# Differential attention: q and k rotated with rows exchanged by transfers within SBUF in place of products with a rotation matrix

## What is computed

```python
def partial_rope(x, cos, sin):            # ROPE_DIM 16 of each 64 channels
    half = ROPE_DIM // 2
    x1 = x[..., :half].astype(jnp.float32)
    x2 = x[..., half:ROPE_DIM].astype(jnp.float32)
    rot = jnp.concatenate([x1 * c - x2 * s, x2 * c + x1 * s], axis=-1)
    return jnp.concatenate([rot.astype(x.dtype), x[..., ROPE_DIM:]], axis=-1)
...
    q = partial_rope(q, cos, sin) * (DH ** -0.5)
    k = partial_rope(k, cos, sin)
...
        s = jnp.einsum('bhcqd,bhckd->bhcqk', q_blk, kt).astype(f32)
        pr = jax.nn.softmax(s, axis=-1)
        pd = pr[:, :, 0] - lam * pr[:, :, 1]
        return jnp.einsum('bhqk,bhkv->bhqv', pd.astype(vt.dtype), vt)
```

## Time and profile before

| | us |
|---|---|
| median of 3 runs (1713.19 to 1714.20) | 1713.61 |
| profiled execution, its own time | 1713.43 |
| its span, first to last instruction | 1711.7 |

### The profile page before, as it was taken

One profiled execution on the slowest core, in us unless ns is written; L12 is line 12 of the kernel. 1 busy time (PEld: TensorE's weight loads), 2 busy tenths in 40 slices (PEclk: granted clock), 3 DMA queues, 4 the chain that ended last, 5 costly groups with the idle time before them and its releaser, 6 DMA issues. The chain is left out here.

```text
span 1711.7 us, 30337 instructions
## 1 busy us (share of the span) xinstructions
PE 1665.2 (97%) x12956; PEld 1305.7 (76%) x12956; DVE 1062.3 (62%) x1509; ACT 725.0 (42%) x1092; POOL 97.0 (6%) x122
## 2 busy tenths in 40 slices
PE   9999999999999999999999999998899999999997
PEld 6666777778767888888888788874477878888887
DVE  6757588878657577576765762327786654343434
ACT  4344555534255443232314553245664553232323
POOL 0000000000000100000111000003100100000001
PEclk9999999999999999999999999999999999999999
DMA  6111231111155344446562232230001223232221
GB/s 220 63 61 68 83 117 40 40 40 47 34 209 185 123 160 147 150 167 212 207 211 77 84 111 62 84 104 0 1 2 62 99 92 106 87 101 97 99 98 50
DMA packets 50165, 171.18 MB, mean 100 GB/s; under 512 B 5600, under 2 KB 9056, under 8 KB 49264
## 3 DMA queue, kind: packets, MB, share of 16 engines
q1 hardware_dynamic: 40272, 133.00, 22.1%
q0 software_dynamic: 9760, 36.25, 6.2%
HBM read 160.84 MB, written 8.39 MB: 99 GB/s over the span
## 5 line engine op out<-in xcount | busy, mean ns | idle before, releaser
L378 PE MATMUL pair<-h_hi,w_hi 128*128 128x512 f32 x1008 | 404.1, 401 | 3.0 <-DVE w_lo L424 2.1
L380 PE MATMUL pair<-h_hi,w_lo 128*128 128x512 f32 x1008 | 392.8, 390 | 0.0
L379 PE MATMUL pair<-h_lo,w_hi 128*128 128x512 f32 x1008 | 392.7, 390 | 0.0
L424 DVE TENSOR_TENSOR w_lo<-w_raw,w_hi 128x1024 fp32r<-128x1024 f32 (+2 forms) x225 | 266.5, 1186 | 172.8 <-ACT w_hi L403 172.6
L403 ACT CAST w_hi<-w_raw 128x1024 fp32r<-128x1024 f32 (+2 forms) x225 | 222.1, 990 | 224.3 <-PE pair L380 219.6
L378 PEld LDWEIGHTS pair<-h_hi,w_hi 128*128 128x128 f32 x1008 | 189.3, 188 | 59.2 <-issue 19.0
L379 PEld LDWEIGHTS pair<-h_lo,w_hi 128*128 128x128 f32 x1008 | 189.4, 188 | 41.0 <-issue 4.1
L380 PEld LDWEIGHTS pair<-h_hi,w_lo 128*128 128x128 f32 x1008 | 189.2, 188 | 40.3
L378 PE MATMUL pair<-ff_f_hi,w_hi 128*128 128x512 f32 (+1 forms) x536 | 204.1, 381 | 0.6 <-DVE w_lo L424 0.6
L380 PE MATMUL pair<-ff_f_hi,w_lo 128*128 128x512 f32 (+1 forms) x536 | 203.5, 380 | 0.0
L379 PE MATMUL pair<-ff_f_lo,w_hi 128*128 128x512 f32 (+1 forms) x536 | 203.5, 380 | 0.0
(11 more groups left out here) (457 smaller groups left out, 2503.4 us busy)
## 6 DMA issues: line engine op xcount, KB each, us to landing
w_raw<-in_w_ff SPq DMA_DIRECT2D x128, 512.0 KB, 3.3
mod_w<-in_w_mod POOLq DMA_DIRECT2D x48, 512.0 KB, 3.7
w_raw<-in_w_in SPq DMA_DIRECT2D x22, 512.0 KB, 3.3
w_raw<-in_w_gate SPq DMA_DIRECT2D x16, 512.0 KB, 3.3
w_raw<-in_w_out SPq DMA_DIRECT2D x16, 512.0 KB, 3.3
w_raw<-in_w_rwkv SPq DMA_DIRECT2D x15, 512.0 KB, 3.2
w_raw<-in_w_da SPq DMA_DIRECT2D x12, 512.0 KB, 4.1
w_raw<-in_w_ple_gate SPq DMA_DIRECT2D x8, 512.0 KB, 3.2
```

The costliest lines, as they stand in the source:

```text
L378: nc.tensor.matmul(out, w_hi, x_hi, start=(k == 0), stop=False)
L379: nc.tensor.matmul(out, w_hi, x_lo, start=False, stop=False)
L380: last = nc.tensor.matmul(out, w_lo, x_hi, start=False, stop=(k == kt - 1))
L424: nc.vector.tensor_tensor(lo[:, s % SPLIT_SLOTS, 0:cols], pr.raw[:, w % RAW_SLOTS, 0:cols], hi[:, s % SPLIT_SLOTS, 0:cols].bitcast(F32), A ...
```

## The change

The eight products with `rot` go, with the matrix and its load. In their place SP copies rows within SBUF: for tile i four transfers of eight rows (16 KB each) bring rows 8 to 15 to 0 to 7, 0 to 7 to 8 to 15, and the same from row 64 on, from the tile into its slot of `turned`. The rest of `turned` is cleared once by GpSimd, ahead of its load of the table. The sign moves into the sine table, which the host lays out. VectorE's sine product reads `turned` and writes it back.

```diff
@@ the tables
+    sin[:, 0:8] *= -1
     out["rope_da"] = per_channel(np.tile(cos, (1, 2)), np.tile(sin, (1, 2)))
@@ DiffAttention
     def load(self, pool):
         nc, dram = self.pr.nc, self.pr.dram
+        for i in range(2):
+            nc.gpsimd.memset(self.turned[:, i, :], 0.0).then_inc(self.s["cleared"], 1)
         pool.dma_start(self.table[:, :, :], dram["rope_da"].rearrange("p (a t) -> p a t", a=2)).then_inc(self.s["table_in"], 16)
 
-    def load_rotation(self, pool):
-        pool.dma_start(self.rot[:, :], self.pr.dram["rot_da"]).then_inc(self.s["rot_in"], 16)
+    def swap(self, sp, i):
+
+        s = self.s
+        sp.wait_ge(s["tile_out"], i + 1)
+        if i < 2:
+            sp.wait_ge(s["cleared"], 2)
+        else:
+            sp.wait_ge(s["roped"], i - 1)
+        for row in (0, 8, 64, 72):
+            sp.dma_start(self.turned[row:row + 8, i % 2, :], self.Q[row ^ 8:(row ^ 8) + 8, DA_ORDER[i], :]).then_inc(s[f"swapped{i % 2}"], 16)
...
@@ DiffAttention.pe, k == 2
-            pe.wait_ge(s["tile_out"], i + 1)
-            if slot > DA_FIRST + 1:
-                pe.wait_ge(s["tr_out"], slot - DA_FIRST - 1)
-            elif i >= 2:
-                pe.wait_ge(s["sin_made"], i - 1 if i == 3 else i)
-            nc.tensor.matmul(self.turn_bank(i), self.rot[:, :], Q[:, DA_ORDER[i], :], start=True, stop=True).then_inc(s["rot_done"], 1)
@@ DiffAttention.pe, k == 6
-            if slot <= 8:
-                pe.wait_ge(s["sin_made"], slot)
-            elif slot <= 12:
+            if 9 <= slot <= 12:
                 pe.wait_ge(s["v_out"], slot - 8)
-            else:
+            elif u:
                 pe.wait_ge(s["tr_out"], u)
@@ DiffAttention.dve
-            dve.wait_ge(s["rot_done"], i + 1)
-            nc.vector.tensor_tensor(self.turned[:, i % 2, :], self.turn_bank(i), self.table[:, 1, :], ALU.mult).then_inc(s["sin_made"], 1)
+            dve.wait_ge(s[f"swapped{i % 2}"], 64 * (i // 2 + 1))
+            nc.vector.tensor_tensor(self.turned[:, i % 2, :], self.turned[:, i % 2, :], self.table[:, 1, :], ALU.mult)\
+                .then_inc(s["sin_made"], 1)
@@ DaIn
     def loads(self, sp):
         self.start_loads(sp)
+        for i in range(2 * DA_HEADS):
+            self.pr.stream(sp, self.jobs[i].weight + 7)
+            self.beside.swap(sp, i)
```

More of the change, by code:

```diff
@@ L88, in shape_constants @@
         "ident64": (i[:, None] % 64 == np.arange(64)[None, :]).astype(f),
-        "rot_da": rope_rotation((64, 8)),
         "rot_att": rope_rotation((64, 32)),
@@ L452, in __init__ @@
         self.sq = [self.table[:, 0, :], self.table[:, 1, :], self.turned[:, 0, :], self.turned[:, 1, :]]
-        self.probT, self.oT, self.rot, self.small, self.lam = (
-            scratch("da_" + k, shape) for k, shape in (("probT", [P, TB, T]), ("oT", [P, 4, T]), ("rot", [P, P]), ("small", [P, 2, 8]),
-                                                       ("lam", [P, 8])))
+        self.probT, self.oT, self.small, self.lam = (
+            scratch("da_" + k, shape) for k, shape in (("probT", [P, TB, T]), ("oT", [P, 4, T]), ("small", [P, 2, 8]), ("lam", [P, 8])))
         self.units = [(h, q) for h in range(DA_HEADS) for q in range(TB)]
         self.s = pr.stage_sems("da_", (
-            "table_in", "rot_in", "tile_out", "rot_done", "sin_made", "cos_made", "roped", "v_done", "v_out", "score", "negmax", "exp", "inv",
+            "table_in", "tile_out", "cleared", "swapped0", "swapped1", "sin_made", "cos_made", "roped", "v_done", "v_out", "score", "negmax", "exp", "inv",
             "scaled", "diff", "tr_done", "tr_out", "pv_done", "o_out", "lam_in", "lam_sum", "lam_exp", "lam_made", "sq", "sum", "log",
@@ L473, in turned_in @@
         return {3: (0, 1), 4: (2, 3), 5: (4,), 6: (5,), 7: (6,), 8: (7,)}.get(slot, ())
-    def turn_bank(self, i):
-        return self.pr.bank[7 if i in (1, 3) else 6]
     def load(self, pool):
         nc, dram = self.pr.nc, self.pr.dram
+        for i in range(2):
+            nc.gpsimd.memset(self.turned[:, i, :], 0.0).then_inc(self.s["cleared"], 1)
         pool.dma_start(self.table[:, :, :], dram["rope_da"].rearrange("p (a t) -> p a t", a=2)).then_inc(self.s["table_in"], 16)
-    def load_rotation(self, pool):
-        pool.dma_start(self.rot[:, :], self.pr.dram["rot_da"]).then_inc(self.s["rot_in"], 16)
+    def swap(self, sp, i):
[7 more added lines that the diff above has]
+            sp.dma_start(self.turned[row:row + 8, i % 2, :], self.Q[row ^ 8:(row ^ 8) + 8, DA_ORDER[i], :]).then_inc(s[f"swapped{i % 2}"], 16)
     def pe(self, pe, slot, k):
@@ L508, in pe @@
             if i == 0:
-                pe.wait_ge(s["rot_in"], 16)
                 pe.wait_ge(s["lam_in"], 2)
                 nc.tensor.matmul(pr.bank[4][:, 0:2], pr.c["ones"], self.lam[:, 0:2], start=True, stop=True).then_inc(s["lam_sum"], 1)
-            pe.wait_ge(s["tile_out"], i + 1)
-            if slot > DA_FIRST + 1:
-                pe.wait_ge(s["tr_out"], slot - DA_FIRST - 1)
-            elif i >= 2:
-                pe.wait_ge(s["sin_made"], i - 1 if i == 3 else i)
-            nc.tensor.matmul(self.turn_bank(i), self.rot[:, :], Q[:, DA_ORDER[i], :], start=True, stop=True).then_inc(s["rot_done"], 1)
         if k == 2 and 9 <= slot <= 12:
@@ L712, in pool @@
     def pool(self, pool):
-        self.beside.load_rotation(pool)
         pool.wait_ge(self.pr.sum_done, 1)
```

## The result

| | us, median (lowest to highest) | profiled execution |
|---|---|---|
| before | 1713.22 (1712.41 to 1714.2), 6 runs | 1713.43, span 1711.7 |
| changed | **1719.73** (1718.47 to 1721.77), 6 runs | 1720.49, span 1718.6 |

Ratio 1.0036, 95% interval 1.0026 to 1.0047: slower by 6.5 us, where 4.4 us less was forecast and the range ended at 1714.2. The prediction was wrong.

What follows compares the result with a forecast made beforehand. TensorE, busy 97% and without a gap in the stage, was taken as the bound: 6.9 us of products removed less 2.5 of new waits gave 4.4 won, 1713.61 to 1709.2 us, range 1705.2 to 1714.2.

Steps and rivals of the forecast that it cites:

- Products removed: Slots 3 to 8 on TensorE: eight rotation products leave its queue, 6.9 us won.
- clears on GpSimd: Two clears ahead of the cosine table's load: table lands between 29.6 and 32.3, costing nothing to 0.3 us, taken as nothing.
- Issue of a swap: SP's queue: four transfers issued 0.45 us apart, so the fourth starts 1.35 us after the first.
- Landing: End of each swap: 2.0 us from issue to landing, taken from the 128 KB load; 1.4 not excluded.
- Swaps 0 to 3 just fit: Slots 3 and 4: first two swaps land at 32.0 and 34.1, just in time; the next two are ready when VectorE comes.
- cushion of 0.2: Scores of slot 6: exponentials end at 46.2, TensorE comes at 46.4, so it need not wait; before, 3.7 us in hand.
- Turn of VectorE: Slots 5 to 8: tile out, swap 3.4, rotation 2.0, differences 1.6, tile out 0.6, together 7.7 us against TensorE's 7.24.
- waits of slots 7 to 9: TensorE waits for exponentials at the scores of these slots: 0.2, 0.45 and 0.45 us.
- The last wait: Slot 10: TensorE's product of head 0 waits 1.4 us for ScalarE's copy of unit 3.
- The clock: Later stretches at 1.2 GHz: a shift can spare or bring one, up to 1.7 us each, widening the range either way.
- Passing through: Later stages start relative to this one, so the gain reaches the end; the rival that it doesn't had 0.05.
- the slower rival: Slots 3 to 8: same chain through the swaps, landing from 3.3 us up, 1715.8 to 1722 us; chance 0.10.

Runs made afterwards that it cites:

- changed kernel with more code: Changed kernel with the warm-up ahead of the program as 12 products of 208 columns instead of 4 of 512: 1717.41 us, ratio 1.002 to the kernel before.
- fillers: Changed kernel plus three unused fp32 products ahead of each of TensorE's two waits (slots 6 and 9): 1715.78 us, ratio 1.0013 to the kernel before.
- 16-row kernel from HBM: Changed kernel with each swap's four 16 KB transfers as 16 rows of 1 KB read from the HBM table, output not the reference's: 1714.76 us, ratio 1.0006.

## Why the prediction was wrong, point by point

**Products removed, 6.9 us:** right; 6.97 by the kernel without swaps, counted from the first tile out. The clears on GpSimd cost nothing, also right: the table is there at 29.34 us, where it was at 29.60 in the kernel before.

**Issue of a swap, 1.35 us from first to fourth:** this term failed. It measured 2.0, since issues that read eight rows of SBUF stand 0.67 apart on SP, and my 0.45 came from loads that read HBM. The upper bound that I allowed, 0.54 for each, was too low as well. **Landing, 2.0:** right (2.0 in slot 5); the 1.4 that I left open below it rested on no row, and none of these kernels shows less than 1.5. (The formula that I quoted beside it, from the Trainium skill, DMA: Bandwidth & Descriptors, under Anatomy of one DMA, is given there for transfers that GpSimd issues, not SP.) The 0.08 us for waking SP was read from no row either; it measured 0.03 (tile out ends at 45.21, the swap starts at 45.24). A swap was 4.0 us, not 3.4.

**Swaps 0 to 3 just fit:** wrong from the same term, and here it counts most. On SP a swap and its weight load come every 3.2 us (31.54, 34.76) where I had 2.1. VectorE waits 0.79, 1.07 and 0.78 us in slots 3 and 4, the exponentials of slot 5 end at 48.43 instead of 46.2, and TensorE waits 2.5 us in slot 6, where I had a cushion of 0.2.

**Turn of VectorE, 7.7:** 8.27. With it the waits of slots 7 to 9 are 1.0 each and not 0.2 to 0.45: seen where the clock was up (changed kernel with more code, fillers), hidden under half rate in the changed kernel.

**The last wait, 1.4 at the product of head 0:** the place was wrong. TensorE needs tile out 8 already at the v transposes of slot 9, a deadline that I had left out. It waits there, 3.1 us. By my own terms it was worth 1.0: tile out 8 ends at 73.6, TensorE starts the scores of slot 9 at 69.2 and is at the transposes some 2.0 us later (67.89 to 69.92 in the 16-row kernel from HBM), so it waits 2.4 there, and the copy of unit 3 at 77.5 is then no longer waited for. With this my sum would have been 3.5 of waiting and 1710.2.

**The clock:** I had the later stretches at half rate as a matter of shift, not that the waits of this very stage would bring two. Worth 1.7 us on top. It is not certain either: with more code TensorE idles 2.49 us ahead of slot 6 and keeps 2.4 GHz. At the barrier of 480 the changed kernel was even spared the half rate, after 3.37 us of idle time where the kernel before had 2.38, and won nothing by it, as it had idled 1.0 longer.

**Passing through:** given 0.05 as a rival of its own and 1.7 us of range; 3.6 us were given back between the landmark and the end. 1.0 to 1.1 of it is the stop that moves with the code, 1.3 the half-rate stretch near 1181, which fell on work with no wait behind it to take it up. The 0.8 behind the barrier at 480 is a wait of TensorE for VectorE's low part; why that comes late stays open: it appears in kernels with and without transfers and with either count. What moves the half-rate stretches stays open too.

**What would have shown it:** the slower rival had the chain right, but hung it on the landing alone, from 2.7 us up. In the sum an issue counts three times per swap and four times in SP's cadence, so 0.2 us more on it did what 0.7 on the landing would have. Together: the forecast was -4.4 and the result +6.5, against the kernel before measured beside it. Of these 10.9 us 7.7 come from the stage (+3.3 against -4.4), and about 3.2 from behind it.

## What to carry to other kernels

Price the issue of a transfer from a row with the same kind of source and target, and count it once for every transfer in the group and for the queue's cadence: where a group sits in a loop between two steps of one engine, the issues count more than the landing. Moving work off the bounding engine onto a queue pays if the result is asked for a slot later: the change made the kernel 6.5 us slower with no lead and 4.8 us faster with one. And when the gain at a landmark behind the edited stage doesn't arrive at the end, look for rows that wait for "issue" inside bursts of short products, and change the number of instructions ahead of them before blaming the edit.

## What the runs showed of the hardware beyond that

An issue of 16 KB on SP, one of four, took 0.66 us for 8 rows within SBUF, 0.60 for 16 or 128 rows within SBUF, 0.43 for 16 rows from HBM and 0.32 for 8 rows from HBM. The weight load right behind such a group, 512 KB from HBM in every kernel, is held up as well: 0.33 us alone (before, and without swaps), 0.44 behind 8 rows within SBUF, 0.58 behind 16 rows, and 0.42 and 0.35 behind 16 and 8 rows from HBM. So an issue has to be priced with what stands ahead of it on the queue. On GpSimd's queue the same 8-row transfer within SBUF took 0.50, with a landing of 1.9. The Trainium skill, DMA: Bandwidth & Descriptors, under Why a DMA increments its semaphore by 16, says that the sequencer itself writes the part of the count that eight rows leave open; had that been the price, 8 rows from HBM would be dearer than 16, and they were the cheapest of all.

Eight more short products ahead of the program moved the whole by -2.3 to +1.2 us, and with them a stop of about 1.0 us moved to another place or went.
